# A transformer kernel whose expert stage builds gates from one-hot matrices: operands in pairs of tokens, made two groups ahead, from piece 47 on

## What is computed

```
s = einsum('thpd,hpnd->thpn', q, sub_keys)          # 8 heads, 2 halves, 128 keys
s1, i1 = top_k(s[:, :, 0], 16); s2, i2 = top_k(s[:, :, 1], 16)
top_s, pos = top_k(s1[..., None] + s2[..., None, :], 16)
idx = take(i1 * 128 + i2, pos); gate = softmax(top_s)
act = gelu(einsum('thkd,td->thk', expert_u[idx], hb))
out = einsum('thk,thkd->td', gate * act, expert_v[idx])
```

## Time and profile before

| | |
|---|---|
| median of 3 runs | 1647.76 us (1646.78 to 1648.29) |
| profiled execution, its own time | 1646.69 us |
| its span | 1644.9 us |
| busy in the span: PE, DVE, ACT, POOL | 1527.0 (93%), 1062.5 (65%), 721.3 (44%), 328.9 us (20%) |
| first matmul of the first group of gates | 946.14 us |
| first matmul of the last group of gates | 1237.44 us |

### The profile page before, as it was taken

How to read it: one execution, slowest core, us unless ns; L and a number is a source line. 1 busy time by engine, 2 the same in 40 slices (tenths; PEclk the granted TensorE clock), 3 DMA queues, 4 the chain that set the end, 5 groups by cost and what they waited for, 6 DMA issues and landing times.

```text
span 1644.9 us, 24838 instructions
## 1 busy us (share of the span) xinstructions
PE 1527.0 (93%) x10282; PEld 1366.1 (83%) x10282; DVE 1062.5 (65%) x1668; ACT 721.3 (44%) x1223; POOL 328.9 (20%) x153
## 2 busy tenths in 40 slices
PE   7997999999988868889999899999999999999998
PEld 6885788998877757869999899999989788888886
DVE  5556555664477877543999567777775555555554
ACT  4563454554355243234544433333334444444443
POOL 0044100000055250358799500000000000000000
PEclk9998999999999889799999999999999999999999
DMA  7622433555543300135555533333335566666663
GB/s 271 204 90 102 138 119 112 182 181 194 190 126 100 114 2 2 39 103 167 185 172 171 179 103 117 117 114 115 116 116 160 174 189 185 190 191 188 186 190 127
DMA packets 64879, 235.25 MB, mean 143 GB/s; under 512 B 7424, under 2 KB 7680, under 8 KB 64512
## 3 DMA queue, kind: packets, MB, share of 16 engines
q1 hardware_dynamic: 63904, 231.60, 44.6%
q10 hardware_dynamic: 864, 2.07, 0.3%
HBM read 232.60 MB, written 1.05 MB: 142 GB/s over the span
## 4 chain that ended last, share of the span: by engine, by line
PE 72%; DVE 15%; ACT 4%; POOL 4%; issue 4%; DMA 1%; ACTq 0%; DVEq 0%; POOLq 0%
PE ps L129 70%; ACT spl L141 3%; POOL spl L144 3%; DVE Ao L144 2%; PE ps L138 1%; DVE spl L144 1%; DVE GE L144 1%; DVE EB L144 1%; DVE junk L144 1%; DVE prep L144 1%; DVE pm L144 1%; DMA raw<-in_w_in_a 1%; DVE be L144 1%; DVE pR L144 1%; DVE pm L153 1%
## 5 line engine op out<-in xcount | busy, mean ns | idle before, releaser
L141 ACT ACTIVATE spl<-raw 128x1024 fp32r<-128x1024 f32 (+1 forms) x435 | 454.9, 1049 | 452.6 <-PE ps L129 435.0
L129 PE MATMUL ps<-xhl,spl 128*128 128x256 f32 x4944 | 611.0, 284 | 11.1 <-POOL spl L144 9.7
L129 PEld LDWEIGHTS ps<-xhl,spl 128*128 128x128 f32 x4944 | 596.8, 190 | 14.5 <-POOL spl L144 11.3
L144 DVE TENSOR_TENSOR spl<-raw,spl 128x1024 fp32r<-128x1024 f32 (+1 forms) x325 | 395.4, 1222 | 289.2 <-ACT spl L141 289.1
L129 PE MATMUL ps<-spl,Wr 128*128 128x512 f32 x1536 | 357.2, 395 | 3.1 <-DVE Wr L144 3.1
L129 PEld LDWEIGHTS ps<-spl,Wr 128*128 128x128 f32 x1536 | 289.3, 188 | 70.8 <-DVE Wr L144 3.3
L144 POOL TENSOR_TENSOR spl<-raw,spl 128x1024 fp32r<-128x1024 f32 (+1 forms) x110 | 283.8, 2597 | 300.5 <-ACT spl L141 300.1
L141 ACT ACTIVATE Wr<-GE 128x256 fp32r<-128x256 f32 x128 | 53.5, 419 | 181.6 <-PE ps L129 181.6
L129 PE MATMUL ps<-Ao,EB 128*128 128x128 bf16 x768 | 100.7, 296 | 17.2 <-DVE Ao L144 17.1
L129 PEld LDWEIGHTS ps<-Ao,EB 128*128 128x128 bf16 x768 | 83.4, 117 | 27.3 <-issue 25.5
L144 DVE TENSOR_TENSOR Wr<-GE,Wr 128x256 fp32r<-128x256 f32 x128 | 54.4, 426 | 79.8 <-ACT Wr L141 79.8
(11 more groups left out here) (337 smaller groups left out, 1248.0 us busy)
## 6 DMA issues: line engine op xcount, KB each, us to landing
raw<-in_eu SPq DMA_DIRECT2D x128, 512.0 KB, 3.6
raw<-in_ev SPq DMA_DIRECT2D x128, 512.0 KB, 4.2
raw<-in_w_up SPq DMA_DIRECT2D x32, 512.0 KB, 3.6
raw<-in_w_down SPq DMA_DIRECT2D x32, 512.0 KB, 3.5
raw<-in_w_in_a SPq DMA_DIRECT2D x16, 512.0 KB, 5.7
raw<-in_w_pq SPq DMA_DIRECT2D x16, 512.0 KB, 3.5
raw<-in_w_rwkv SPq DMA_DIRECT2D x14, 512.0 KB, 3.5
raw<-in_w_in_t SPq DMA_DIRECT2D x8, 512.0 KB, 3.6
```

The lines of the kernel that those rows point to most:

```text
L129: return Done(self, self.e and self.e.matmul(out, l, r, start=st, stop=sp))
L141: return Done(self, self.e and self.e.activation(out, a, f, bias=bias, scale=scale, accum_out=acc))
L144: return Done(self, self.e and self.e.tensor_tensor(out, a, b, op))
```

## The change

Four edits.

1. `EB`, `Ao` and the iota are laid out in pairs of tokens: the inner run is 2 elements where it was 4, so that the step between one token's elements is 4 bytes where it was 8. Each of the two operations of `onehots` becomes two of half the size; the two comparisons stand first, then the two products.
2. DVE makes the one-hot operands of group g + 2 right behind `gate_scored(g)`, ahead of `gate_chunk`; before, it made those of g + 1 behind `gate_chunk`.
3. From piece `GATES` to the end of the loop ACT evaluates Gelu of piece c first and splits piece c + 3 then; before, and still for the earlier pieces, the other way round.
4. The choice's second part begins behind piece 42 (before: 46), the groups of gates run beside pieces 47 to 110 (before: 51 to 114), and DVE makes low parts from piece 44 on (before: 48).

The hunks are, in order: the constants, the tiles, PE (`gates`, its loop), ACT (`scores`, its loop), DVE (`onehots`, its loop).

```diff
-EU_POOL = 48
-GATES, NGRP = 51, 64
+EU_POOL = 44
+CHOICE, GATES, NGRP = 42, 47, 64
...
-        EB = SE("EB", [128, 2, 2, 128, 4], BF16)
+        EB = SE("EB", [128, 2, 2, 2, 128, 2], BF16)
...
-        Ao = SO("Ao", [128, 2, 3, 128, 4], BF16)
-        io4 = SO("io4", [128, 128, 4], BF16)
+        Ao = SO("Ao", [128, 2, 3, 2, 128, 2], BF16)
+        io2 = SO("io2", [128, 128, 2], BF16)
...
-                        last = pe.mm(b[:, q * 128:q * 128 + 128], EB[:, g % 2, 1, :, q], Ao[:, g % 2, k, :, q], k == 0, k == 2)
+                        last = pe.mm(b[:, q * 128:q * 128 + 128], EB[:, g % 2, 1, q // 2, :, q % 2], Ao[:, g % 2, k, q // 2, :, q % 2], k == 0, k == 2)
...
-                if c == 48:
+                if c == CHOICE + 2:
...
-                w.past("eu", c)
+                if not n:
+                    w.past("eu", c)
                 act.wait_ge("w_used", AT["eu"] + c)
...
                 x.then_inc("ge", c)
+                w.past("eu", c)
...
-                if c == 46:
+                if c == CHOICE:
...
-                eb, ao = EB[:, g % 2, :, :, :], Ao[:, g % 2, :, :, :]
-                dve.after(dve.tt(eb, bc(io4[:, :, :], 1, 2), bc(idx[:, :, ts], 2, 128), ALU.is_equal).own())
-                x = dve.tt(ao, bc(eb[:, 0, :, :], 1, 3), bc(gp[:, :, ts], 2, 128), ALU.mult)
+                eb, ao = EB[:, g % 2, :, :, :, :], Ao[:, g % 2, :, :, :, :]
+                pair = lambda t, a: bc(t[:, :, 4 * g + 2 * a:4 * g + 2 * a + 2], 2, 128)
+                made = [dve.tt(eb[:, :, a, :, :], bc(io2[:, :, :], 1, 2), pair(idx, a), ALU.is_equal).own() for a in range(2)]
+                for a in range(2):
+                    dve.after(made[a])
+                    x = dve.tt(ao[:, :, a, :, :], bc(eb[:, 0, a, :, :], 1, 3), pair(gp, a), ALU.mult)
                 x.then_inc("Ao", g)
...
                 if GATES <= c < GATES + NGRP:
                     gate_scored(c - GATES)
+                if GATES <= c + 2 < GATES + NGRP:
+                    onehots(c + 2 - GATES)
                 if c > GATES:
                     gate_chunk(c - 1)
-                if GATES <= c + 1 < GATES + NGRP:
-                    onehots(c + 1 - GATES)
                 w.past("eu", c)
-                if c == 46:
+                if c == CHOICE:
...
-                if c == 49:
+                if c == CHOICE + 2:
```

More of the change, by code:

```diff
@@ L2464, in vector @@
             dve.wait_ge("h4")
-            dve.cp(io4[:, :, :], bc(C("iota"), 2, 4)).own()
+            dve.cp(io2[:, :, :], bc(C("iota"), 2, 2)).own()
             ch = [choose(0), choose(1)]
```

## The result

The changed kernel takes 1579.99 us (median of 4 runs, 1579.24 to 1580.35) against 1647.27 us before (4 runs): the ratio is 0.960, 95% interval 0.9585 to 0.9610. It is faster by 67 us, twice what was forecast (32 us) and outside the range of 1608 to 1628.

What follows compares the result with a forecast made beforehand. The prediction took operands stuck behind a waiting low part as the bound; removing this gave 29.2 us, plus 3.4 at the start, minus 0.3: 32.3 us off 1646.69, 1615.5 as median, range 1608 to 1628.

Steps and rivals of the forecast that it cites:

- Pairs on PE: Gate matmuls on PE: going from a step of 8 bytes to 4 was claimed to gain 0.
- rival C: Gate matmuls on PE: the step matters, a group is 0.35 us shorter, 22 us more gained, 1593 us; chance 0.10.
- The loop: Gates stage: next operands stand behind a low part waiting for the previous piece; 8.94 us for two pieces, 4.47 each.
- PE's own 4.16 us: PE's work per period in the gates stage: 1.32 us for a group plus 2.84 for an eu piece.
- DVE: One-hot operands on DVE: paired halves keep the full rate, taking 412 and 548 ns.
- rival B: DVE becomes the bound as repeated pairs read slower: 1653 us, chance 0.07; smaller factor, 1618 to 1630, another 0.07.
- the spare time of 0.8 us a period: DVE in the gates stage: 4.16 less 3.36 us of work leaves 0.8 us spare in a mean period.
- The start: First group of gates: PE waits 1.2 instead of 4.66 us, 3.4 gained, and the clock stays up.
- The price of 2.2 us: Start of the gates in the kernel before: cost of the lower clock behind PE's idle stretch, counted as gained.
- The end: Change to the ev pieces: Gelu ahead of the split makes PE wait longer, charged 0.3 us.
- Rival D: Gates stage: another wait, something on ACT, keeps half of the lost 0.46 us; 15 us less gained, 1630; chance 0.10.

Runs made afterwards that it cites:

- step2: Changed kernel with PE reading 128 elements in a row (step 2 bytes) as both operands, so gates are wrong and only times count: 1575.9 us.
- set_step8: Changed kernel with only the stationary operand `EB` laid out at a step of 8 bytes again: 1580.9 us, ratio 0.9609 to the kernel before.
- pairs_only: Kernel before the change with the pair layout alone (one-hots in four operations): 1624.2 us, ratio 0.987.
- one_ahead: Changed kernel with the operands made one group ahead and behind `gate_chunk` again: 1628.0 us, ratio 0.990 to the kernel before.
- no_pairs: Changed kernel with the old layout (step 8 bytes) and two one-hot operations, the other edits kept: 1620.5 us, ratio 0.985 to the kernel before.

## Why the prediction was wrong

- **The step that failed**: "*Pairs on PE* ... so the step does not seem to cost anything: 0". It costs 12 x 54 ns = 0.65 us a group, 42 us in 64 groups. With it (and the 0.1 below) the period of 4.16 becomes 3.61, and 64 x (4.16 - 3.61) = 35 us is just what the forecast of 1615.5 lacks. The argument compared bf16 matmuls at step 8 with f32 matmuls of the same size without gaps and found the same 110 ns. Two different limits happened to agree: bf16 without gaps takes 54 ns (step2). What holds the f32 ones at 113 was not tried; but the eu pieces' f32 matmuls, of twice the columns, take 118 ns (2.84 / 24), so already in the rows of before 113 ns was no price for 128 columns. The formula of the Trainium skill that the prediction sets beside rival C ("TensorE: Matmul & The Clock Gate", "LDWEIGHTS (loading the stationary operand)", columns over 1.2) gives 107 ns for a weight load. That this was near 109 was a coincidence: a weight load with step 8 goes along at 60 ns (set_step8).
- **Rival C had the mechanism with a bound that was too high**: 80 ns from twice a matmul of 64 columns, also an f32 one. With the 0.65 us measured its sum would have been 1615.5 - 42 = 1574, and 1580 with the 0.1 us that the pieces take longer. The 81 ns that the prediction quotes there from the Trainium skill ("TensorE: Matmul & The Clock Gate", "Back-to-back issue gap") are not what the trace shows either: 56 ns.
- **A page on the step**: "SBUF — State Buffer" of the Trainium skill, in the note on cachelines of its section "Door 1: The DMA port swizzle", asks for at least two hits on a line of 16 bytes for full bandwidth, and gives 8 bf16 elements as the stride that is free. The trace disagrees with both for the moving operand: two hits a line (a step of 8 bytes) take twice the time of four, and a stride of 8 elements (16 bytes) four times. Lines of 16 bytes do agree with the nearly equal holds at 16 and 24.
- **The loop was right.** Undoing edit 2 brings the wait for `Ao` back and making it takes the wait away; the periods of pairs_only, 4.28 us (expected 4.3), and one_ahead, 4.38 (expected 4.5), agree with the rows of one turn of the loop.
- **A term mis-sized**: PE's own 4.16 us. An eu piece holds PE for 2.84 us among its like and for 2.92 to 2.94 beside a group, in the kernels with steps up to 8 bytes where PE never waits inside the stage (3.03 at 16 and 24 bytes, at full clock). Why is not shown. no_pairs, which is my forecast as a kernel, has a period of 4.26 and 1620.5 us instead of 1615.5.
- **DVE was right**: 419 and 552 ns, no loss of rate with a repeated pair, so rival B is wrong. The two statements that the prediction takes from the Trainium skill ("Vector Engine (DVE) Microarchitecture Reference") pull apart here: its rule on runs of two adjacent words (section "Measured stream behaviour on trn2"), by which the operands would have taken 2.5 us, does not show in an operand that repeats one word; the trace, (552 - 419) / 256 = 0.52 ns an element, agrees with what section 5.1 says of a row read again and again. But the spare time of 0.8 us a period was reckoned against 4.16. Against 3.61 it is nothing at the end of the stage, where DVE is busy 36.19 of 36.20 us, and DVE waits for a high part in 33 of the periods, not in each. PE does not wait, for the operands are two groups ahead.
- **The start was right**: 1.2 us of wait and no stretch at the lower clock. The reading of that clock in the kernel before was not: 0.83 on the mean of 20 us is 20 x 0.17 / 0.5 = 6.8 us at 1.2 GHz, not 3.4. The price of 2.2 us stands, for it came from the durations of two pieces, and the group in front lost nothing at half the clock. **The end** was charged 0.3 us; the wait grew by 0.2, and the clock took 1.4 more.
- **Rival D** did not come: no wait of PE took the place of the one removed.

## What to carry to other kernels

Price a matmul by a row with the same element type and the same access pattern; where none exists, its lower bound is the number of columns at the full clock, not the nearest row that has another limit. Look at the step of the moving operand in bytes: here every byte from 4 to 16 was paid in full. When a loop between engines and the work of the engine it holds are both shortened, run each alone too: 22 and 26 us became 66.

## What was not expected of the hardware

- The moving operand's step: 54, 56, 84, 108, 220 and 210 ns for 128 bf16 columns at 2, 4, 6, 8, 16 and 24 bytes. The stationary operand's step of 8 bytes cost at most 4 ns a matmul.
- A group at step 8 held PE for 1.33 us at half the clock and 1.32 at the full one; a group at step 4 for 1.20 and 0.67.
- f32 matmuls of this size without gaps held PE for 113 ns, twice what bf16 ones do.
- Behind PE's wait at the ev pieces came 3.4 us or more at 1.2 GHz in all eleven kernels that waited 3.3 us, and in one of the three that waited 3.14 us. What decides it there is open.
